# Task order of one attention stage, its side work's steps, and chunk pairs of a two-block transformer kernel on one core

## The reference

```
for l in range(DEPTH):                      # first_block, DEPTH = 2
    proj = rms_norm(x, attn_norm[l]) @ w_in[l]
    h_mla, h_diff, h_ch = jnp.split(proj, [IN_MLA, IN_MLA + IN_DIFF], axis=-1)
    o_mla = rms_norm(mla_attention(h_mla, ...), mla_out_norm[l])
    o_diff = diff_attention(h_diff, ...)
    o_ch = rms_norm(chunk_attention(h_ch, ...), chunk_out_norm[l])
    x = x + jnp.concatenate([o_mla, o_diff, o_ch], axis=-1) @ w_out[l]
    x = x + conv_ffn(rms_norm(x, ffn_norm[l]), ...)
...
# mla_attention, 6 heads
    c_q, c_kv, k_r = jnp.split(h, [MLA_Q_RANK, MLA_Q_RANK + MLA_KV_RANK], axis=-1)
    q = rms_norm(c_q, q_norm) @ w_uq        # rope on the last 32 columns of a head
    kv = rms_norm(c_kv, kv_norm) @ w_ukv    # keys (nope part) and values
    k_rope = apply_rope(k_r, cos, sin)      # one for all heads
# diff_attention, 6 heads of two maps each
    p = jax.nn.softmax(s, axis=-1)
    a = p[:, 0] - lam_full * p[:, 1]
# chunk_attention, 4 heads: softmax(q k * scale + bias) v, a band of 9 chunks of 64
```

## Time and profile before

| | |
|---|---|
| median of 3 runs | 2953.73 us (2952.84 to 2956.28) |
| the profiled execution: its own time | 2954.29 us |
| its span | 2952.6 us |
| attention stage of layer 0 in it | from 61.7 to 250.3 us |
| attention stage of layer 1 in it | from 710 to 898 us |
| busy: PE, DVE, ACT, POOL | 2879.6, 1354.4, 846.2, 1364.3 us |
| mean granted clock of TensorE | 0.992 |

### The profile page before, as it was taken

The page is one execution under the profiler, slowest core; times in us unless marked ns, Lnnn a source line. Parts: engine busy times, 40 slices in busy tenths (PEclk is TensorE's granted clock), DMA queues, the critical chain, the costliest instruction groups (busy, mean ns, idle before and its releaser), DMA issues.

```text
span 2952.6 us, 40774 instructions
## 1 busy us (share of the span) xinstructions
PE 2879.6 (98%) x14054; PEld 2384.2 (81%) x14054; DVE 1354.4 (46%) x2969; ACT 846.2 (29%) x1893; POOL 1364.3 (46%) x924
## 2 busy tenths in 40 slices
PE   8989999999999999999999999999999999999998
PEld 6768888878778888879888878888798888788886
DVE  6476525254476524355773541112547734511124
ACT  3364312122373212122553230001225532300112
POOL 4322555554213555555233645555453336455553
PEclk9999999999999999999999999999999999999999
DMA  7323555565323655656333755565463336555653
GB/s 262 115 86 101 190 194 192 192 207 175 104 72 134 204 194 178 206 188 204 108 121 123 223 169 194 187 201 194 150 200 115 115 122 222 170 194 190 199 192 109
DMA packets 136521, 494.17 MB, mean 167 GB/s; under 512 B 15280, under 2 KB 15536, under 8 KB 136112
## 3 DMA queue, kind: packets, MB, share of 16 engines
q0 software_dynamic: 66240, 241.20, 25.3%
q1 hardware_dynamic: 68544, 245.40, 24.7%
q10 hardware_dynamic: 1584, 5.46, 0.5%
HBM read 489.91 MB, written 2.10 MB: 167 GB/s over the span
## 4 chain that ended last, share of the span: by engine, by line
PE 93%; DVE 2%; issue 2%; ACT 1%; DMA 1%; POOL 0%; SPq 0%; POOLq 0%; DVEq 0%; ACTq 0%
PE ps L573 22%; PE ps L574 22%; PE ps L575 22%; PE ps L601 4%; PE ps L597 4%; PE ps L598 4%; PE ps L844 2%; PE ps L796 2%; PE ps L770 2%; PE ps L720 1%; PE ps L721 1%; PE ps L722 1%; PE ps L836 1%; PE ps L784 1%; DMA w_hi<-weights 1%
## 5 line engine op out<-in xcount | busy, mean ns | idle before, releaser
L546 POOL TENSOR_TENSOR w_lo<-w_raw,w_hi 128x1024 fp32r<-128x1024 f32 x460 | 1108.3, 2409 | 139.0 <-DMA w_hi<-weights 129.8
L573 PE MATMUL ps<-hi,w_hi 128*128 128x512 f32 x2716 | 1073.5, 395 | 1.4 <-POOL w_lo L546 1.2
L574 PE MATMUL ps<-hi,w_lo 128*128 128x512 f32 x2716 | 1062.1, 391 | 0.0
L575 PE MATMUL ps<-lo,w_hi 128*128 128x512 f32 x2716 | 1062.0, 391 | 0.0
L541 POOL DMA_DIRECT2D w_hi<-weights x460 | 261.4, 568 | 1414.9 <-PE ps L575 1001.0
L573 PEld LDWEIGHTS ps<-hi,w_hi 128*128 128x128 f32 x2716 | 512.7, 189 | 115.7 <-issue 11.2
L575 PEld LDWEIGHTS ps<-lo,w_hi 128*128 128x128 f32 x2716 | 512.0, 188 | 108.4
L574 PEld LDWEIGHTS ps<-hi,w_lo 128*128 128x128 f32 x2716 | 512.6, 189 | 100.3 <-issue 1.0
L597 PE MATMUL ps<-hi,w_hi 128*128 128x512 f32 x500 | 197.6, 395 | 5.9 <-POOL w_lo L546 3.9
L598 PE MATMUL ps<-hi,w_lo 128*128 128x512 f32 x500 | 195.9, 392 | 0.0
L2047 ACT ACTIVATE ps<-hb,col 128x512 f32<-128x512 f32 x88 | 68.6, 782 | 381.2 <-DVE hb L1195 381.2
(11 more groups left out here) (352 smaller groups left out, 3617.7 us busy)
## 6 DMA issues: line engine op xcount, KB each, us to landing
w_raw<-weights SPq DMA_DIRECT2D x460, 512.0 KB, 4.2
w_hi<-weights POOLq DMA_DIRECT2D x460, 512.0 KB, 4.6
x<-xt SPq DMA_DIRECT2D x8, 256.0 KB, 10.2
out<-x SPq DMA_DIRECT2D x8, 256.0 KB, 2.0
kc<-k ACTq DMA_DIRECT2D x1, 1346.0 KB, 6.2
bias<-relb ACTq DMA_DIRECT2D x2, 512.0 KB, 5.1
bias<-relb ACTq DMA_DIRECT2D x1, 1024.0 KB, 4.8
praw<-pt ACTq DMA_DIRECT2D x2, 512.0 KB, 6.2
```

The costliest lines, as they stand in the source:

```text
L546: nc.gpsimd.tensor_tensor(wlo[s][:, :], raw[s][:, :], whi[s][:, :].bitcast(F32), ALU.subtract).then_inc(w_split, 1)
L573: nc.tensor.matmul(out_ap, w[0], xx[0], start=first, stop=False)
L574: nc.tensor.matmul(out_ap, w[1], xx[0], start=False, stop=False)
L575: return nc.tensor.matmul(out_ap, w[0], xx[1], start=False, stop=last)
```

## The change

The tasks of `attention_1` run as `d + c + m`. The full tiles run in a new order, one in each two steps from 0 to 23, without the pause that steps 15 and 16 had. `AT_SPREAD` goes to 24 and `AT_KR` to 29, and what hangs on them goes along; the second burst of key copies goes from step 28 to 33. The MLA items go to steps 28 to 46 with gaps, in a new order whose last is `Q5`. MLA tasks are scored in pairs, and since two tasks of a pair can differ in width, each map carries its own. On DVE the reductions of both tasks of a group come in the even step, the second behind the combination and ahead of the normalisation. The sums of squares of the outputs are taken in another order. And all chunk pairs get a `lead` of six, or of four where the source has six chunks (as in the last group of the first block's feed-forward); that of the first layer's start keeps its two. `dense` is as it was, so a call with a lead of six waits for the first unit, runs six chunks of tile one, waits for the second unit, runs six chunks of tile two and then two pairs. The diff, without moved lines that stay as they were (the DVE function `scores_out` holds the reduction's loop of before, word for word, for task `i`):

```diff
-FULL = ["cq0", "ck0", "cc0", "cc1", "cc2", "dq1", "dk1", "kr", "dq2", "dk2", "cq1", "ck1"]
-ITEM_AT = {24: "Q0", 25: "K0", 26: "Q1", 27: "V0", 28: "V1", 29: "Q2", 30: "Q3", 31: "K1", 32: "Q4", 33: "Q5", 34: "K2",
...
+ITEM_AT = {28: "Q0", 29: "K0", 31: "V0", 32: "Q1", 34: "V1", 35: "V2", 37: "V3", 38: "Q2", 40: "K1", 41: "Q3", 43: "Q4",
...
+FULL = ["dq1", "dk1", "cc0", "cc1", "cc2", "dq2", "dk2", "kr", "cq0", "ck0", "cq1", "ck1"]
...
-                                   ss=24 + 6 * qb + h, group=1, accum=h >= 4, value=tile_1(l, f"V{qb}") if h == 0 else None, **more))
-            return d[0:8] + c_[0:8] + d[8:24] + c_[8:16] + m_
+                                   ss=24 + 6 * qb + h, group=2 - 2 * (qb % 2), accum=h >= 4, value=tile_1(l, f"V{qb}") if h == 0 else None, **more))
+            return d + c_ + m_
...
-        QUARTERS.update({0: 2 - AHEAD_1, 14: 4, 15: 0, 16: 0, 17: 4})
-        FULL_END = [1, 3, 5, 7, 9, 11, 13, 14, 17, 19, 21, 23]
...
+        QUARTERS.update({0: 2 - AHEAD_1})
+        FULL_END = list(range(1, 24, 2))
...
-        AT_STATS, AT_SPREAD, AT_KR = 12, 15, 20
+        AT_STATS, AT_SPREAD, AT_KR = 12, 24, 29
...
-            return [dn[0], cn[0], dn[1], dn[2], mn[0], mn[1]]
+            return dn + [cn[0], mn[0], mn[1]]
...
-                        maps = [m for u in ts[it + 1:it + 1 + t.more["group"]] for m in u.maps]
+                        maps = [(lq, rk, u.n) for u in ts[it + 1:it + 1 + t.more["group"]] for lq, rk in u.maps]
...
-                        for lq, rk in maps:
-                            last = nc.tensor.matmul(ps[:, S_BANK_1[q.s % 4], 0:t.n], lq, rk, start=True, stop=True)
+                        for lq, rk, cols_n in maps:
+                            last = nc.tensor.matmul(ps[:, S_BANK_1[q.s % 4], 0:cols_n], lq, rk, start=True, stop=True)
...
-                dense(2, A, NC_, need, 0 if l else 2)
+                dense(2, A, NC_, need, NC_ - 2 if l else 2)
...
-                    done = (w_used, 3) if name == "V3" else (part_done, 1)
+                    done = (w_used, 3) if name == LAST_ITEM else (part_done, 1)
...
-                    if name == "V3":
+                    if name == LAST_ITEM:
...
-                        dense(2, B, NC_, need)
+                        dense(2, B, NC_, need, NC_ - 2)
...
-                    dense(8, A, g, fneed)
+                    dense(8, A, g, fneed, g - 2)
...
-                dense(3, B, NC_, need)
+                dense(3, B, NC_, need, NC_ - 2)
...
-                        dense(8, B, NC_, fneed)
+                        dense(8, B, NC_, fneed, NC_ - 2)
                     else:
-                        dense(3, B, NC_, fneed)
+                        dense(3, B, NC_, fneed, NC_ - 2)
...
+                def scores_out(i):
+
...
                 for it in range(n + 4):
-                    if it < n:
...
+                    if it < n and it % 2 == 0:
+                        scores_out(it)
...
+                    if it < n and it % 2 == 0:
+                        scores_out(it + 1)
...
-                    if k == 1:
+                    if k < 3:
+                        to = ss[:, 8 * k:8 * k + 8].rearrange("p (h q) -> p q h", h=2)
+                    elif k == 3:
                         to = by_head(ss[:, 48:64])[:, :, 0:2]
-                    elif k < 4:
-                        i = (0, None, 1, 2)[k]
-                        to = ss[:, 8 * i:8 * i + 8].rearrange("p (h q) -> p q h", h=2)
...
-                    elif ITEM_AT.get(it - 1, " ")[0] == "Q":
+                    if ITEM_AT.get(it - 1, " ")[0] == "Q":
                         name = ITEM_AT[it - 1]
-                        dve.wait_ge(part_done, q.part + list(ITEM_AT).index(it - 1) + 1)
+                        if name == LAST_ITEM:
+                            dve.wait_ge(w_used, q.unit + 3)
+                        else:
+                            dve.wait_ge(part_done, q.part + list(ITEM_AT).index(it - 1) + 1)
...
-                    elif it == AT_FACTOR:
...
+                    if it == AT_FACTOR:
...
-                    elif it - 1 in ITEM_AT:
+                    if it - 1 in ITEM_AT:
...
-                        if name == "V3":
-                            act.wait_ge(w_used, q.unit + len(FULL) + 3)
-                        else:
+                        if name != LAST_ITEM:
                             q.part += 1
-                        if kind in "KV" and name != "V3":
+                        if kind in "KV":
...
-                    elif it == AT_FACTOR:
+                    if it == AT_FACTOR:
...
-                    if it in (AT_KR + 2, 28):
+                    if it in (AT_KR + 2, AT_KR + 4):
...
-                        for h in ((0, 1), (2, 3, 4, 5))[it == 28]:
+                        for h in ((0, 1), (2, 3, 4, 5))[it == AT_KR + 4]:
```

More of the change, by code:

```diff
@@ L76 @@
 N_K2 = 2564
[L80 to L84 removed]
+ITEM_AT = {28: "Q0", 29: "K0", 31: "V0", 32: "Q1", 34: "V1", 35: "V2", 37: "V3", 38: "Q2", 40: "K1", 41: "Q3", 43: "Q4",
+           44: "K2", 46: "Q5"}
+LAST_ITEM = "Q5"
+ORDER_1 = ["dq1", "dk1", "cc0", "cc1", "cc2", "dq2", "stats", "dk2", "kr", "cq0", "ck0", "cq1", "ck1", "sp0", "sp1",
+           *ITEM_AT.values()]
+FULL = ["dq1", "dk1", "cc0", "cc1", "cc2", "dq2", "dk2", "kr", "cq0", "ck0", "cq1", "ck1"]
 TILES_1 = 4 + len(ORDER_1) + 8 + 2 * FF1_C + 8 * len(FF1_GROUPS)
@@ L1199, in attention_1 @@
                 on0 = q.on
[L1200 to L1215 removed]
+                def scores_out(i):
+                    t, pb = ts[i], slots(i)[0]
+                    for m in range(len(t.maps)):
+                        s = q.s
+                        dve.wait_ge(s_done, t.scored)
+                        if m:
+                            if q.pair >= 2:
+                                dve.wait_ge(p_ready, t.p0 - 1)
+                            q.pair += 1
+                        elif i >= 4:
+                            dve.wait_ge(t_done, t.id - 3)
+                        V.tensor_tensor_reduce(out=pb[4 + i % 2 if m else i % 4][:, 0:t.n], in0=ps[:, S_BANK_1[s % 4], 0:t.n],
+                                               in1=t.more["add"], scale=-t.scale, scalar=3.0e38, op0=ALU.add, op1=ALU.min,
+                                               accum_out=ngm(s)).then_inc(s_free, 1)
+                        q.s += 1
+                for it in range(n + 4):
+                    if it < n and it % 2 == 0:
+                        scores_out(it)
                     if 1 <= it <= n:
```

17 lines of the change are left out of this document (removed).

## The result

| | before | after |
|---|---|---|
| median (range, runs) | 2953.85 us (2952.84 to 2962.94, 7) | 2942.22 us (2937.61 to 2947.36, 7) |
| ratio of the runs, 95% interval | | 0.9948 [0.9937, 0.9959] |
| the profiled execution: its own time, span, mean clock | 2954.29, 2952.6, 0.992 | 2937.61, 2935.9, 0.995 |

The changed kernel is faster by 11.6 us at the medians. The same kernel on a second chip gave 2937.22 us against 2957.77 (0.9925 [0.9905, 0.9945]). So the size depends on the executions by several us, and the experiments show where these come from.

A forecast was written before the change was run, and what follows sets the result against it. PE, busy 98%, was taken to bound the kernel, so only its waits and clock count. Per layer -6.7 - 3.1 - 1.0 - 0.5 + 4.5 + 1.0 + 1.2 = -4.6; twice, plus 6.7 once, -15.9: 2938 us, range 2928 to 2948.

The forecast's parts named there:

- the last rival: Longer lead does nothing, because the second unit is late anyway or the clock falls all the same: 2944 us; chance 0.06.
- The start of layer 1: First chunk pair of layer 1: longer lead removes PE's idle gap and slow clock, gaining 6.7 us once (6.0 to 6.7).
- Waits before scores: Attention steps 17, 19 and 21: three PE waits behind DVE's reductions and the slow clock go, 6.7 us a layer.
- Items: MLA items spread over steps 24 to 36 find their bank empty, so 3.1 us of waits a layer go.
- The table load: Square root's table load stalls a transpose; K2 and Q5 now stand around it, gaining 1.0 us a layer.
- New waits in steps 24 to 31: MLA preparation lands where no full tile covers it; PE waits for DVE, costing 4.5 us a layer (3.4 to 7.8).
- Key copies: Steps 32 to 39: four key copies on ACT at step 33 delay transposes, costing 1.0 us a layer (0 to 2.5).
- MLA pairs: MLA scores in pairs: fewer switches, but transposes wait for ACT; loss 1.2 us a layer (gain 0.8 to loss 4).
- The last item: Frees three weight slots ten steps later (46 instead of 36); loads stay hidden before the out projection at step 64.
- That DVE takes it all back: Preparation costs at steps 24 to 31 what it cost at 15 to 23; only the layer start gains: 2950; chance 0.15.
- That it goes better: DVE works ahead, new waits only 3.4, key copies cost nothing, pairs gain 0.8 a layer: 2930; chance 0.08.
- That the clock stays low over steps 24 to 39: Without full tiles, PE's idle pieces keep the granted clock at 1.2 GHz: +24 us a layer, 2986; chance 0.03.

The follow-up runs named there:

- single scores: Changed kernel with the MLA tasks scored one by one instead of in pairs: 2953.33 us, ratio 0.9987 to the kernel before.
- packed items: Changed kernel with the thirteen MLA items one each step from 28 to 40, same order: 2950.47 us, ratio 0.9976 to the kernel before.
- own steps: Changed kernel with each of DVE's score reductions in the task's own step, as before the change: 2931.38 us, ratio 0.9917 to the kernel before.
- own steps and single scores: Changed kernel with each reduction in its own step and MLA tasks scored one by one: 2927.16 us, ratio 0.9889 to the kernel before.
- own steps, single scores, statistics at 14 and later factors: Changed kernel, reductions in own step, MLA scored singly, MLA chunk statistics at step 14 instead of 12, DVE's output factors at 46 instead of 45: 2924.16 us.
- the last item at 45: Kernel with reductions in own step, MLA scored singly, statistics at 14, factors at 46, plus last item Q5 at step 45 instead of 46: 2927.37 us.

## Why the prediction was right, point by point

**The total.** 2938 was forecast, from 15.9 us less. The profiled execution gave 16.7 less, the ratio 15, the medians 11.6. Of the 15.9 the prediction counted 6.0 as the clock's (1.7 in each layer's attention stage, 2.6 at the start of layer 1). Over the whole span the low clock cost 22.3 us before and 15.6 in the changed kernel's first trace, but 22.3 again in its second. So the clock gave 6.7 us in one execution and nothing in the other, and without it the change is worth 10.0 and 13.3 us of span, where the prediction had 9.9. The waits were forecast well, then, but that the profiled execution came within 1 us of 2938 was luck; the first chip's median lies 4 us above it, nearer to the last rival's 2944.

**The start of layer 1.** Right in mechanism, in the units' times (the second split ends 3.8 us behind the start of the last matmul of layer 0, where it was 4.1) and, against the profile, in size: 6.65 of 6.7. As a mean it is probably too large: the run without the lead shows that 3.2 of it were a low clock that does not always come.

**Waits before scores, 6.7 a layer with the clock.** They went, as forecast. But the cause was named as the place of the preparation alone, and the early reduction was said to only help. The runs show that either removes these waits, and that early reductions delay normalisations for which products wait. In the changed kernel as it is, moving the preparation is worth 0.3 to 1.7 us a layer; without early reductions and pairs, 3.1. *The step that failed: "Hoisting the odd task's reduction ahead of the normalisation frees score banks earlier and can only help here."* In its place the runs show 7 us a layer of cost with single scores, and with pairs 0.3 to 1.4 us of waits. The same prediction noted, under what comes, that both reductions stand ahead of a normalisation for which a product waits, and priced it in steps 24 to 31 alone.

**Items, 3.1.** Right: packed items bring back 4.5 us of waits before them and lengthen the rest by 2.1 to 4.5.

**The table load, 1.0, and the rest of the waits before scores, 0.5.** The 1.5 us before a transpose are not in the changed kernel's list (its longest there is 0.4), and come back with packed items; right.

**New waits in steps 24 to 31, 4.5 (3.4 to 7.8).** Measured 3.2, just under the lower end; 2.3 with own steps. No DVE operation was stretched: the split of the unit released at step 23 ran beside the spread, on POOL's timeline of the changed kernel, and was over 5 us before the low halves:

```profile
161.78 2.36 POOL L547 TENSOR_TENSOR w_lo<-w_raw,w_hi 128x1024 fp32r<-128x1024 f32 x1
```

```profile
169.63 1.28 DVE L1130 TENSOR_TENSOR mlo<-tmp,mhi 128x512 fp32r<-128x512 f32 x2
```

So 1.28 for two, where the earlier trace rows had 2.59, and the 1.4 us that the rule of the prediction would have added did not come.

**Key copies, 1.0.** The burst of four takes 2.18 us on ACT at step 33, and waits of 0.20 and 0.60 follow (the second behind DVE, which waits for ACT's exponential until 188.02): 0.8.

**MLA pairs, 1.2 (-0.8 to 4).** Right in sign by the traces: 2.0 beside own steps. The run with single scores alone pointed the other way, and was an interaction.

**The last item, priced at nothing.** Its loads stay hidden, as said. What was missed is that the split of the third unit lands on a scaling of DVE: 2.29 us instead of 0.67 in the changed kernel, with 0.51 us of wait behind it, and 1.5 in the kernels with own steps and single scores. The Trainium skill (SBUF — State Buffer, "Who interferes with whom") says that a DVE instruction with two SBUF inputs and a reading GpSimd instruction exclude each other for the whole instruction; the trace agrees, since DVE's 2.54 us end 0.55 us behind POOL's split. The prediction used this rule at one place and not at the other.

**The rivals.** That DVE takes it all back came near in one form only: the changed kernel with single scores is as slow as before. That it goes better, 2930, did not come for this kernel (2942.22 and 2937.22). That the clock stays low over steps 24 to 39 did not come, but a part of it did: one stretch there in each layer of the second trace. That the lead does nothing is not excluded by the times (0.9991 with it alone, 0.9957 without it against 0.9948 with it); the traces show 3.5 us.

## What to carry to other kernels

Where one engine bounds by its own work, look at which of two queued operations the bound engine waits for first: an early reduction frees a bank and delays whatever is queued behind it, and which counts changes with the way in which the scores are grouped. Undo parts one at a time and in pairs: single scores alone cost 11 us, while with own steps they shorten each layer's stage by 2. When an event that frees buffers is moved, follow it to the work that it starts on another engine (here a split on POOL) and ask what that collides with.

## What was not expected of the hardware

The granted clock fell to its lower level (0.5, 1.2 of 2.4 GHz) at different places in two executions of the same kernel, behind waits and at the small matmuls of the statistics, and what it cost in a stage was 0.0, 1.7, 3.4, 5.1 or 6.8 us. More waits did not always mean more of it: own steps, single scores, statistics at 14 and later factors lost 0.0 and 1.7 us in the two stages and packed items 6.8 and 6.8, but the kernel with the last item at 45, whose stages hold the fewest waits (5.4 us), lost 6.8 and 3.4. So the times moved by more than the waits: on one chip the profiled execution with packed items was 13.9 us longer than that of the changed kernel; the two attention stages hold 4.6 and 3.5 of these, and 5.6 lie ahead of the first scores, where the two kernels are the same (3.4 of them are the clock's). What decides, behind a given wait, whether the clock falls was not tried. The executions of the kernel before spread from 2949.5 to 2963.9 us over 21 runs, so that a change of 3 us is seen in a trace sooner than in the times.
